# The first two tiles of each projection share the wait for their last contraction block

## The reference

```
h = concat(meta, x)
layer A: h += diff_attention(rms_norm(h)) @ w_o        # 8 heads, two score maps each
         h += (silu(conv3(a)) * b) @ w_out             # a, b = split(rms_norm(h) @ w_in); 2816 wide
layer B: h += latent_attention(rms_norm(h)) @ w_o      # 16 heads, compressed keys and values
         h += (silu(conv3(a)) * b) @ w_out
h = rms_norm(h)[:, 16:]
layer C: p = rms_norm(h) @ w_in + b_in                 # 47 tiles of 128 columns
         merged = sigmoid(gc) * (conv part @ w_conv_out) + sigmoid(ga) * (window attention @ w_attn_out + b)
         h += merged @ w_mix_out
         h += (silu(conv3(a)) * b) @ w_out
out = rms_norm(h)
```

## Time and profile before

| | us |
|---|---|
| device time, median of three runs | 2309.8 |
| lowest and highest run | 2308.52, 2311.93 |
| span of the profiled execution | 2309.6 |
| TensorE busy | 2196.9 (95%) |
| DVE busy | 1348.9 (58%) |
| ScalarE busy | 784.3 (34%) |
| POOL busy | 870.5 (38%) |

### The profile page before, as it was taken

One profiled execution on the slowest core, in us unless ns is written; L12 is line 12 of the kernel. 1 busy time (PEld: TensorE's weight loads), 2 busy tenths in 40 slices (PEclk: granted clock), 3 DMA queues, 4 the chain that ended last, 5 costly groups with the idle time before them and its releaser, 6 DMA issues.

```text
span 2309.6 us, 39350 instructions
## 1 busy us (share of the span) xinstructions
PE 2196.9 (95%) x14044; PEld 1926.8 (83%) x14044; DVE 1348.9 (58%) x2068; ACT 784.3 (34%) x1407; POOL 870.5 (38%) x349
## 2 busy tenths in 40 slices
PE   7999889999999899999999999899999989999997
PEld 6788789999999877769999999877778868788785
DVE  6666756526346867763665726876641275627374
ACT  3333434323223355552422222324442223322222
POOL 3332234434344311113444444444334444534442
PEclk9998999999999999999999999999999999999998
DMA  4111122222222201112222222322222332222321
GB/s 166 65 64 64 55 67 86 86 92 91 82 82 92 91 29 37 36 37 78 82 92 92 91 82 82 100 82 83 70 86 92 100 109 87 95 91 91 100 83 72
DMA packets 52503, 188.25 MB, mean 82 GB/s; under 512 B 5825, under 2 KB 5953, under 8 KB 52417
## 3 DMA queue, kind: packets, MB, share of 16 engines
q1 hardware_dynamic: 51408, 185.16, 24.2%
q10 hardware_dynamic: 1008, 1.89, 0.2%
HBM read 184.93 MB, written 2.10 MB: 81 GB/s over the span
## 4 chain that ended last, share of the span: by engine, by line
PE 86%; DVE 10%; issue 2%; ACT 2%; DMA 0%; DVEq 0%; SPq 0%; ACTq 0%
PE ps L447 25%; PE ps L448 25%; PE ps L449 25%; PE ps L569 3%; PE ps L606 3%; PE ps L608 2%; DVE g_hi L811 1%; PE ps L588 1%; DVE g_lo L813 1%; DVE scratch L1012 1%; DVE scratch L854 1%; PE ps L592 1%; DVE x_hi L804 1%; PE ps L760 1%; PE ps L483 1%
## 5 line engine op out<-in xcount | busy, mean ns | idle before, releaser
L430 POOL TENSOR_TENSOR w_lo<-w_raw,w_hi 128x1024 fp32r<-128x1024 f32 x345 | 870.3, 2531 | 1413.9 <-ACT w_hi L1374 1374.5
L447 PE MATMUL ps<-x_hi,w_hi 128*128 128x264 f32 (+2 forms) x2760 | 886.2, 321 | 10.1 <-DVE scratch L1339 5.7
L448 PE MATMUL ps<-x_lo,w_hi 128*128 128x264 f32 (+2 forms) x2760 | 872.9, 316 | 0.0
L449 PE MATMUL ps<-x_hi,w_lo 128*128 128x264 f32 (+2 forms) x2760 | 871.8, 316 | 0.0
L447 PEld LDWEIGHTS ps<-x_hi,w_hi 128*128 128x128 f32 x2760 | 525.9, 191 | 56.3 <-issue 8.0
L448 PEld LDWEIGHTS ps<-x_lo,w_hi 128*128 128x128 f32 x2760 | 525.6, 190 | 33.5 <-issue 1.0
L449 PEld LDWEIGHTS ps<-x_hi,w_lo 128*128 128x128 f32 x2760 | 525.4, 190 | 32.8
L1374 ACT ACTIVATE w_hi<-w_raw 128x1024 fp32r<-128x1024 f32 x345 | 358.9, 1050 | 328.8 <-PE ps L449 326.1
L447 PE MATMUL ps<-g_hi,w_hi 128*128 128x264 f32 (+2 forms) x1312 | 415.7, 317 | 40.5 <-DVE g_lo L813 38.8
L448 PE MATMUL ps<-g_lo,w_hi 128*128 128x264 f32 (+2 forms) x1312 | 413.6, 315 | 0.0
L449 PE MATMUL ps<-g_hi,w_lo 128*128 128x264 f32 (+2 forms) x1312 | 412.6, 314 | 0.0
(11 more groups left out here) (166 smaller groups left out, 1738.9 us busy)
## 6 DMA issues: line engine op xcount, KB each, us to landing
w_raw<-stream SPq DMA_DIRECT2D x345, 512.0 KB, 3.3
h<-x_t SPq DMA_DIRECT2D x4, 528.0 KB, 8.5
out_t<-h SPq DMA_DIRECT2D x8, 256.0 KB, 2.1
scratch<-rotary_tables ACTq DMA_DIRECT2D x4, 264.0 KB, 5.6
par<-params ACTq DMA_DIRECT2D x1, 342.5 KB, 5.0
scratch<-positions ACTq DMA_DIRECT2D x1, 256.0 KB, 2.8
cst<-shape_constants ACTq DMA_DIRECT2D x1, 193.0 KB, 6.6
```

The lines of the kernel that those rows point to most:

```text
L430: nc.gpsimd.tensor_tensor(w_lo[:, j % 4, :], w_raw[:, j % 4, :], w_hi[:, j % 4, :].bitcast(F32), ALU.subtract).then_inc(lo_ready, 1)
L447: nc.tensor.matmul(out_ap, w_hi[:, s, c], xh[:, k, cols], start=first, stop=False)
L448: nc.tensor.matmul(out_ap, w_hi[:, s, c], xl[:, k, cols], start=False, stop=False)
L449: return nc.tensor.matmul(out_ap, w_lo[:, s, c], xh[:, k, cols], start=False, stop=last)
```

## The change

The first two tiles of a projection are run together. Each does all its blocks but the last, in both banks; then TensorE waits for the last operand block, and finishes tile 0 and tile 1. It holds for WO, the attention B output, CO, AO, MX and the nine down projections, 14 in all, not for the up projections. As only six tiles are left, the loop of `tiles` isn't used there any more and all eight are written out.

```diff
                                       b == 0, b == blocks - 1)
                 last.then_inc(half_done, 1)
 
-            def tiles(j, tl, n, blocks, xh, xl, T, ready, after_first=None):
+            def tile_pair(j, tl, blocks, xh, xl, T, ready):
+
+                for m in range(2):
+                    pe.wait_ge(lo_ready, j + m + 1)
+                    wait(pe, tile_taken, tl + m - 1)
+                    for bank, t0, n in chunks(T):
+                        for b in range(blocks - 1):
+                            if not m and not bank:
+                                pe.wait_ge(ready[0], ready[1] + b + 1)
+                            passes(ps[:, 2 * ((j + m) % 2) + bank, 0:n], j + m, b, xh, xl, b, slice(t0, t0 + n),
+                                   b == 0, False)
+                pe.wait_ge(ready[0], ready[1] + blocks)
+                for m in range(2):
+                    for bank, t0, n in chunks(T):
+                        last = passes(ps[:, 2 * ((j + m) % 2) + bank, 0:n], j + m, blocks - 1, xh, xl, blocks - 1,
+                                      slice(t0, t0 + n), False, True)
+                    last.then_inc(half_done, 1)
+
+            def tiles(j, tl, n, blocks, xh, xl, T, ready, after_first=None, paired=False):
 
                 done = 0
+                if paired:
+                    tile_pair(j, tl, blocks, xh, xl, T, ready)
+                    done = 2
                 if after_first:
                     tile(j, tl, blocks, xh, xl, T, ready)
                     after_first()
...
                     j, tl = j + 2 * g, tl + 2 * g
-                    tiles(j, tl, KD, g, g_hi, g_lo, T, (g_ready, g0))
+                    tiles(j, tl, KD, g, g_hi, g_lo, T, (g_ready, g0), paired=True)
...
-            tiles(J_WO, TL_WO, KD, KD, g_hi, g_lo, T1, (g_ready, G_WO))
+            tiles(J_WO, TL_WO, KD, KD, g_hi, g_lo, T1, (g_ready, G_WO), paired=True)
...
-            tiles(J_BO, TL_BO, KD, KD, g_hi, g_lo, T3, (g_ready, G_BO))
+            tiles(J_BO, TL_BO, KD, KD, g_hi, g_lo, T3, (g_ready, G_BO), paired=True)
...
-            tiles(J_CO, TL_CO, KD, KD, g_hi, g_lo, T2, (g_ready, G_CO))
-            tiles(J_AO, TL_AO, KD, 4, x_hi, x_lo, T2, (x_ready, X_AO))
-            tiles(J_MX, TL_MX, KD, KD, g_hi, g_lo, T2, (g_ready, G_MX))
+            tiles(J_CO, TL_CO, KD, KD, g_hi, g_lo, T2, (g_ready, G_CO), paired=True)
+            tiles(J_AO, TL_AO, KD, 4, x_hi, x_lo, T2, (x_ready, X_AO), paired=True)
+            tiles(J_MX, TL_MX, KD, KD, g_hi, g_lo, T2, (g_ready, G_MX), paired=True)
```

## The result

The changed kernel took 2272.2 us (median of 4 runs, 2271.8 to 2273.5) beside 2310.3 us (2308.5 to 2311.9) for the kernel before: ratio 0.9834, 95% interval 0.9822 to 0.9846. The forecast was 2269.0 with a range of 2259 to 2282, so it came out as its likeliest case had it, 3.2 us slower. Up to WO all kernels with POOL's whole subtraction have the same code, and yet WO starts between 295.6 and 299.7 us in their profiled executions, so kernels whose medians differ by less than that are told apart by their stages. One execution of one variant (a single pair) took 4221 us and is left out.

The account below looks back on a forecast made before the run. TensorE's matmul stream was taken to bound the kernel (86% of the span). 54.2 - 5.1 - 4.6 - 1.5 - 0.7 - 1.5 = 40.8 us, taken from 2309.8, gave 2269.0 us, range 2259 to 2282.

Parts of the forecast that it names:

- CO, AO, MX: One DVE-bound chain that the pair in AO and CO's gap make 2.6 us later; net -1.5 us.
- The waits and the clock go together: WO and the down projections: idle waits for the last operand and slow-clock stretches after them both go, 54.2 us gained.
- Rival (b): In the projections, idle time goes but most of 17 us of clock loss stays: about 2284 us, chance 0.12.
- The gap: At tile 2, TensorE waits until DVE has taken tile 0: 0.53 us, or 0.47 at 512 columns; together 5.1 us.
- The row of the takes that was forecast: Line 447 waiting for lines 824, 900, 868, 1334 and 1339: some 13 waits, mostly 0.2 to 0.4 us.
- rival (d): Tile 1 of the pairs can't run ahead, so idle time stays and gaps are added: 2310 to 2315 us, chance 0.03.
- Rival (c): One POOL subtraction holds up the take of tile 0 at each of 14 pairs: slower, 2322 us, chance 0.05.
- Feed-forward 1's third, the cut for DVE: Third down projection: DVE lags, TensorE waits at the next stage's first tile; 3.2 us gained instead of 7.8.
- Rival (a): DVE keeps pace in the third projections, so the cuts of 4.6, 1.5 and 0.7 fall away: 2263 us, chance 0.20.
- the 0.7 us charged for feed-forward 1's first projection: First down projection of feed-forward 1: angle operations beside two subtractions may hold up tile 3, -0.7 us.
- Feed-forward 0's third: Third down projection, leading into a DVE-bound stage: POOL's lock of DVE cuts the 6.9 us gain by 1.5 us.

Follow-up runs that it names:

- The fill experiment: Kernel before with 30 useless matmuls ahead of the last-operand wait in the six down projections of feed-forward 0 and 1: 2299.6 us.
- the fitted versions: Changed kernel, no pair in CO, AO, attention B output, fewer blocks ahead elsewhere: 2268.7 us; also none ahead in feed-forward 0's third: 2264.2 us.

## Why the prediction was right, and where it was off

Each step by its net value, the sum of its terms in the prediction beside the stages:

| step | forecast | measured |
|---|---|---|
| WO | 5.4 | 5.4 |
| feed-forward 0, first two | 11.0 | 10.8 |
| feed-forward 0, third, to attention B | 4.9 | -0.2 |
| attention B output | -0.5 | -0.5 |
| feed-forward 1, first two | 10.5 | 11.4 |
| feed-forward 1, third, to CO | 3.2 | 3.1 |
| CO, AO, MX | -1.5 | -2.0 |
| feed-forward 2, first two | 3.1 | 2.9 |
| feed-forward 2, third | 4.8 | 4.5 |
| sum | 40.9 | 35.4 |

The spans differ by 37.9 us, 2.5 more than the column: most of it, some 2 us, is a shorter end of attention B. It isn't the pairs: the kernel before with the matmuls of no use, which has none, has the same (230.45 us of attention B beside 232.53 before and 230.50 after). That the total came within 3.2 us of the forecast is so in part luck: the steps alone give 5.5 us less than forecast.

- *The waits and the clock go together.* Right. Line 447's waits for `g_lo` are 0.6 us (forecast below 3), the granted clock is 1.00, and a down projection of feed-forward 0 takes 47.58 and 47.24 (forecast 47.3). The fill experiment shows the clock part by itself. Rival (b) falls. One of the arguments against it was misread, though: behind AO's wait that ends at 1851.63 three matmuls do come as at full clock, but from the fourth on they are at half clock, in the kernel before:

```profile
1852.46 0.63 PE L447 MATMUL ps<-x_hi,w_hi 128*128 128x512 f32 x1
```

  So a wait of 2.1 us did cost clock there. The gaps of 0.2 to 0.6 us at tile 2 did not, with 1.00 as the granted clock of the down projections.
- *The gap.* 0.47 us in the second down projection, as against 0.53; the one at 512 columns held too (0.49 to 0.51, forecast 0.47). Inside the 0.53, 0.19 was charged for the second matmul, which is its whole distance; over the pace of 0.12 it is 0.08 (0.20 measured), and the wait before it costs 0.39 where 0.34 was forecast. The row of the takes that was forecast doesn't exist by name; they are in the row "issue", 13 as forecast. With one block less the gap closes, so it is the take. The pairs do run ahead as written, so rival (d) is out. Rival (c), the take locked by POOL, falls: the takes at line 845 beside POOL last 0.70.
- *Feed-forward 1's third, the cut for DVE.* The size was right, 3.1 against 3.2, but not all of its path: DVE's last take is 5.2 us ahead of before (4.8 forecast), and TensorE doesn't wait 5 us for `x_lo` at the next stage. It waits for takes already inside the projection and at its end, 1.43, 1.37 and 1.40 us, because a tile's banks come free at DVE's pace; then 0.9 for `x_lo` and 1.8 for an accumulation behind it. The clock falls for none of them. The prediction had put the whole wait at the next stage. Rival (a), that DVE keeps pace, falls with this and the next point; only the 0.7 us charged for feed-forward 1's first projection didn't come (it takes 46.34 us, the second 46.41).
- *Feed-forward 0's third.* This is the step that failed. The prediction put a cut of 1.5 us on it, from an average of lock per tile. In fact the pair puts DVE and POOL into a fixed phase in which every second tile's `x_hi` and `x_lo` are blocked; the projection isn't held up by it (35.92 us, at full clock), but TensorE then waits 4.8 us for its last operand, as I had forecast for the end of feed-forward 1. Behind that a second meeting with POOL, at line 1218, makes TensorE wait 4.2 us where it waited 1.6, and attention B starts at the same distance as before. The term was -1.5 and measured -6.6. Without the lockstep 1.3 us of it come back (96.84 to 95.55 in the fitted versions); why the pair brings the second meeting about is open. The view of waits in the earlier trace rows was read for what comes late before the projection; what the projection feeds was only read for feed-forward 1.
- *CO, AO, MX.* Right in direction and nearly in size (-2.0 for -1.5). AO alone is 2.5 longer, for the reason given; 1.0 of it is its matmuls, 25.81 us busy for 24.79, at a lower clock. MX wins 1.0 back.

## What to carry to other kernels

A stall of TensorE for one late operand costs its idle time and the clock after it, and reordering its own work so that something else is there to do gets both back, as long as nothing downstream takes them; hold back no more blocks than the wait is long, since results that arrive in pairs reach the next engine in bursts. Before reordering around a late operand, look at why it is late: here it was DVE blocked behind POOL's 2.5 us instructions, and cutting these into four brought 43 us on top of the fitted pairs, which had brought 47. With POOL's instruction short, the pairs of the change were worth 0.7 us instead of 38. A gain in a stage counts from the stage's start to the next point where both kernels wait for the same thing, not within the stage.

## What the runs showed of the hardware that I had not expected

- A POOL subtraction of 1024 columns takes 2535 ns, two of 512 take 1456 each, four of 256 take 842 each (means of their groups): POOL's busy time grows from 871 to 1115 us, and the kernel becomes 43 us faster, because DVE's operations fit between the pieces (DVE 1143 us busy instead of 1362).
- The lock has phases. The same instructions at the same rate settle into a rhythm without a blocked operation (`x_hi` 0.50, `x_lo` 0.77) or into one with two of four blocked (1.78 and 2.85). In these runs it went with the time between the first two takes: 2.8 or 2.9 us apart (five and two blocks ahead) gave the second rhythm, 5.9 us (none ahead) the first.
- Matmuls of no use during a wait paid: five of the six down projections that had them became 1.4 to 1.9 us shorter, the sixth 0.9, because the granted clock stayed up.
